# Samples' attention scores in two column halves, and the scan's output finished in its own chunk

## The reference, cut to what matters

```python
# samples (DEC_BATCH 8, DEC_SEQ 4, 16 heads of 64): attention over the cached keys and the new ones
logits = einsum('bthd,btjhd->bthj', q, kg) * ATTN_SCALE + bias
m = max(logits); pr = exp(logits - m); den = sum(pr)
o = einsum('bthj,btjhd->bthd', pr, vg) / den[..., None]

# prompt: state-space scan in chunks of 128 tokens (8 chunks), 16 heads of 64, state 128, 2 groups
y_diag = einsum('bcijgr,bcjgrp->bcigrp', cb[..., None] * decay * dtc[:, :, None], xc)
y_off  = einsum('bcign,bcigr,bcgrpn->bcigrp', cc, exp(cum), h_prev)
y = (y_diag + y_off) + xs * d_skip[:, None]
y = y.reshape(b, t, D_SSM) * silu(z)
yg = y.reshape(b, t, 2, D_SSM // 2)
yg = yg * rsqrt(mean(yg * yg, axis=-1, keepdims=True) + EPS)
h = x + concat(attn_o, yg * ssm_norm) @ w_out
y = h + square(relu(rmsnorm(h) @ w_up)) @ w_down
```

## Time and profile before

| | |
|---|---|
| runs | 2103.23, 2101.59, 2103.22 us, median 2103.22 |
| profiled execution, own time | 2098.7 us |
| its span, first to last instruction | 2096.9 us |
| PE busy | 1998.9 us (95%) |
| DVE, ACT, POOL busy | 1031.3, 699.6, 941.6 us |
| mean granted TensorE clock | 0.987 of full speed |

### The profile page before, as it was taken

The page is one execution under the profiler, slowest core; times in us unless marked ns, Lnnn a source line. Parts: engine busy times, 40 slices in busy tenths (PEclk is TensorE's granted clock), DMA queues, the critical chain, the costliest instruction groups (busy, mean ns, idle before and its releaser), DMA issues.

```text
span 2096.9 us, 30132 instructions
## 1 busy us (share of the span) xinstructions
PE 1998.9 (95%) x11992; PEld 1820.7 (87%) x11992; DVE 1031.3 (49%) x1355; ACT 699.6 (33%) x1194; POOL 941.6 (45%) x580
## 2 busy tenths in 40 slices
PE   8999999988888999899999999999999999999999
PEld 7999998777777888565567799999999999999998
DVE  4888803877767666477777561521212212121212
ACT  5344323666556676555552021210010101010010
POOL 4688613777657665234332123233332323232332
PEclk9999999999999999999999999999999999999999
DMA  4444435453343442878755423011111111111112
GB/s 168 149 190 160 149 113 127 115 121 101 87 112 95 117 132 81 267 258 277 232 210 191 172 99 126 31 51 41 51 40 50 40 50 41 49 40 50 40 50 93
DMA packets 117925, 239.36 MB, mean 114 GB/s; under 512 B 29995, under 2 KB 63659, under 8 KB 116284
## 3 DMA queue, kind: packets, MB, share of 16 engines
q1 hardware_dynamic: 94956, 205.69, 30.4%
q10 hardware_dynamic: 22864, 32.25, 4.7%
HBM read 187.78 MB, written 58.67 MB: 118 GB/s over the span
## 4 chain that ended last, share of the span: by engine, by line
PE 65%; DVE 7%; ACT 6%; issue 4%; POOL 1%; DMA 0%; ACTq 0%; DVEq 0%; SPq 0%; POOLq 0%
PE wo_psa L2377 9%; PE wo_psa L2395 9%; PE wo_psb L2377 9%; PE wo_psb L2395 7%; PE dense_ps L966 6%; PE wo_psa L2225 4%; PE sa_s L1512 3%; PE wo_psb L2329 2%; PE wo_psa L2329 2%; DVE att_p L1071 1%; PE att_t_ps L995 1%; ACT att_p L1165 1%; PE ssd_in L1616 1%; PE att_s_ps L984 1%; ACT att_qhi L1182 1%
## 5 line engine op out<-in xcount | busy, mean ns | idle before, releaser
L913 POOL TENSOR_SCALAR att_p<-att_p,att_rden 128x128 f32<-128x128 f32 (+7 forms) x128 | 251.0, 1969 | 132.6 <-DVE att_rden L1053 132.6
L2134 POOL CAST wo_hi<-wo_raw 128x1024 fp32r<-128x1024 f32 x64 | 66.7, 1042 | 496.8 <-issue 242.1
L2492 ACT ACTIVATE r_sq<-stage 128x1056 f32<-128x1056 f32 x32 | 34.8, 1089 | 625.1 <-DVE stage L2693 625.1
L2136 POOL TENSOR_TENSOR wo_lo<-wo_raw,wo_hi 128x1024 fp32r<-128x1024 f32 x64 | 185.3, 2895 | 5.1
L1058 DVE TENSOR_TENSOR att_pTlo<-att_t_ps,att_pThi 128x512 fp32r<-128x512 f32 x192 | 106.3, 554 | 112.1 <-ACT att_pThi L1173 110.6
L2377 PE MATMUL wo_psb<-mix_split,wo_hi 128*128 128x352 f32 x768 | 144.9, 323 | 0.0
L2377 PE MATMUL wo_psa<-mix_split,wo_hi 128*128 128x352 f32 x768 | 144.2, 322 | 0.0
L1173 ACT ACTIVATE att_pThi<-att_t_ps 128x512 fp32r<-128x512 f32 x192 | 93.4, 487 | 127.9 <-PE att_t_ps L995 120.7
L966 PE MATMUL dense_ps<-u_hi,w_hi 128*128 128x352 f32 x480 | 117.8, 347 | 16.4 <-DVE conv_pre L1085 7.8
L2377 PEld LDWEIGHTS wo_psb<-mix_split,wo_hi 128*128 128x128 f32 x768 | 128.3, 188 | 0.5 <-issue 0.5
L2377 PEld LDWEIGHTS wo_psa<-mix_split,wo_hi 128*128 128x128 f32 x768 | 128.0, 188 | 0.0
(11 more groups left out here) (315 smaller groups left out, 5148.0 us busy)
## 6 DMA issues: line engine op xcount, KB each, us to landing
sa_k<-in_cache_k SPq DMA_DIRECT2D x32, 640.0 KB, 7.6
sa_v<-in_cache_v SPq DMA_DIRECT2D x40, 512.0 KB, 4.7
w_raw<-in_w_feat SPq DMA_DIRECT2D x36, 512.0 KB, 6.3
wo_raw<-in_w_up SPq DMA_DIRECT2D x32, 512.0 KB, 3.5
wo_raw<-in_w_down SPq DMA_DIRECT2D x32, 512.0 KB, 3.5
out_qk<-proj_out SPq DMA_DIRECT2D x16, 528.0 KB, 7.9
tmp_bias_rows<-tmp_table ACTq DMA_DIRECT2D x8, 1024.0 KB
att_bias<-tmp_bias_rows SPq DMA_DIRECT2D x16, 512.0 KB, 3.2
```

Of the source, the lines that this page charges most:

```text
L913: pool.tensor_scalar(slot(h, qt), slot(h, qt), rden[:, qt, :], None, ALU.mult).then_inc(normed, 1)
L2136: pool.tensor_tensor(w_lo[:, j], raw_w, w_hi[:, j].bitcast(F32), ALU.subtract).then_inc(f_split[j], 1)
```

## The change

- **Scores in two column halves.** Pair f = 2u goes to rows 0 to 63 of `s_ps`, pair 2u+1 to rows 64 to 127, which are the upper 64 columns of PE's array. The column piece is the outer loop now, so the two matmuls that follow each other write different halves. The number of matmuls and their sizes are the same. `softmax_min` adds the halves: one more DVE operation, a `tensor_tensor` of 64 x 672 that adds the upper rows to the bias, ahead of the old one.
- **y in its own chunk.** `turn_y(n, g)`, `add_skip(n, g)`, `gate(n)`, `square(n)`, `sum_squares(n)` stand in iteration n, not n+1; `skip_x(n)` comes earlier on POOL. Nothing of chunk 7 but `sum_squares`, `norm_sums` and `keep_norm` is left for the head of `outward`.
- **Order.** `norm_sums(n-1)` moves between the scores and `sample_gather(n-1)` behind them; on DVE `keep_own(n-1)` opens the iteration and `softmax_min(n)` stands ahead of `keep_norm` and `keep_out`; on ACT the first two of the four `segment` calls of chunk n+1 stand ahead of `exponent(n)`, the last two behind `square(n)`; SP loads z first and the rows of decays one chunk further ahead.
- **Reciprocals.** `keep_norm` has no reciprocal. Eight reciprocals of 128 x 256 stand in `outward` at q = 8, 10, ..., 22, behind the square root, and `scale` moves to q = 25, 29, ..., 53.

```diff
@@ sync
-                if n >= 1 and n + 1 < NC:
-                    load_rows(n + 1)
+                if n:
+                    load_z(n)
                 if n + 1 < NC:
                     load_k(n + 1)
-                if n:
-                    load_z(n)
+                if n + 2 < NC:
+                    load_rows(n + 2)
@@ tensor
-                for i in range(KP):
-                    f = u * KP + i
-                    for c, w in ((0, 512), (512, NKEYS - 512)):
-                        mm = pe.matmul(s_ps[0:R, c:c + w], q_diag[:, f, :], kT[:, u, i, c:c + w],
-                                       start=(f == 0), stop=(f == NPAIR - 1))
+                for c, w in ((0, 512), (512, NKEYS - 512)):
+                    for i in range(KP):
+                        f = u * KP + i
+                        mm = pe.matmul(s_ps[i * R:(i + 1) * R, c:c + w], q_diag[:, f, :], kT[:, u, i, c:c + w],
+                                       start=(f < KP), stop=(f >= NPAIR - KP))
...
                 if n:
                     sample_scores(n, 1)
+                    sample_scores(n, 2)
+                    norm_sums(n - 1)
+                    sample_scores(n, 3)
                     sample_gather(n - 1)
-                    turn_y(n - 1, 0)
-                    sample_scores(n, 2)
-                    turn_y(n - 1, 1)
-                    sample_scores(n, 3)
...
                 sample_values(n, 1)
+                turn_y(n, 0)
...
                 sample_values(n, 3)
-                if n:
-                    norm_sums(n - 1)
+                turn_y(n, 1)
                 sample_values(n, 4)
@@ gpsimd
+                skip_x(n)
                 if n + 1 < NC:
                     place(n + 1)
-                if n:
-                    sum_squares(n - 1)
-                if n + 1 < NC:
                     weigh_x(n + 1)
-                if n + 1 < NC:
-                    skip_x(n)
+                    sum_squares(n)
@@ scalar
                 for t in range(VS):
                     cast_v(n, t)
+                if n + 1 < NC:
+                    segment(n + 1, 0)
+                    segment(n + 1, 1)
                 if n:
-                    square(n - 1)
                     exponent(n)
...
-                    for q in range(4):
-                        segment(n + 1, q)
+                square(n)
+                if n + 1 < NC:
+                    segment(n + 1, 2)
+                    segment(n + 1, 3)
@@ vector
-                dve.wait_ge(norm_kept, n + 1)
-                dve.reciprocal(part, part)
...
-                dve.tensor_tensor_reduce(out=probs[:, 0:NKEYS], in0=s_ps[0:R, 0:NKEYS], in1=bias[:], scale=1.0, scalar=3e38,
-                                         op0=ALU.add, op1=ALU.min, accum_out=low[:]).then_inc(biased, 1)
+                dve.tensor_tensor(probs[:, 0:NKEYS], s_ps[R:2 * R, 0:NKEYS], bias[:], ALU.add).then_inc(biased, 1)
+                dve.wait_ge(biased, 2 * b + 1)
+                dve.tensor_tensor_reduce(out=probs[:, 0:NKEYS], in0=s_ps[0:R, 0:NKEYS], in1=probs[:, 0:NKEYS], scale=1.0,
+                                         scalar=3e38, op0=ALU.add, op1=ALU.min, accum_out=low[:]).then_inc(biased, 1)
@@ outward
-    SCALE_AT = {9 + 6 * k: k for k in range(KD)}
+    INVERT_AT = {8 + 2 * i: i for i in range(8)}
+    SCALE_AT = {25 + 4 * k: k for k in range(KD)}
...
+            def invert_root(i):
+                part = y_sums[:, i // 4, i % 4 * 2 * P:(i % 4 + 1) * 2 * P]
+                dve.wait_ge(y_rooted, 2)
+                dve.reciprocal(part, part).then_inc(y_rooted, 1)
```

More of the change, by code:

```diff
@@ L1672, in _ @@
                 sample_values(n, 3)
-                if n:
-                    norm_sums(n - 1)
+                turn_y(n, 1)
                 sample_values(n, 4)
-            pe_tail = turn_y, sample_gather, norm_sums
-            mixed.pe_tail = pe_tail
+            mixed.pe_tail = sample_gather, norm_sums
         @block.gpsimd
@@ L1762, in _ @@
                     kit.clear(pool)
-            mixed.pool_tail = skip_x, sum_squares
+            mixed.pool_tail = sum_squares
         @block.scalar
@@ L1970, in _ @@
                     split_v(n, 1)
+                    softmax_min(n)
+                    keep_norm(n - 1)
                     keep_out(n - 1)
-                    add_skip(n - 1, 0)
-                    add_skip(n - 1, 1)
-                    gate(n - 1)
-                    split_v(n, 2)
-                    softmax_min(n)
                 add_state(n, 0)
@@ L1986, in _ @@
                     split_v(0, 1)
-                    split_v(0, 2)
+                split_v(n, 2)
+                if n == 0:
                     split_new()
-                split_v(n, 3)
                 if n + 1 < NC:
                     mask_cb(n + 1)
+                add_skip(n, 0)
+                split_v(n, 3)
+                add_skip(n, 1)
                 split_v(n, 4)
-                if n + 1 < NC:
-                    mix(n + 1, 0)
-                if n + 1 < NC:
-                    keep_own(n)
-                    mix(n + 1, 1)
-                    scale_off(n + 1, 0)
-                    if n:
-                        keep_norm(n - 1)
-            mixed.dve_tail = keep_own, add_skip, gate, keep_out, keep_norm
+                gate(n)
+            mixed.dve_tail = keep_own, keep_out, keep_norm
     return mixed
@@ L2106, in _ @@
         def _(pool):
-            skip_x, sum_squares = mixed.pool_tail
+            sum_squares = mixed.pool_tail
             pool.wait_ge(mixed.k_used, mixed.scores)
@@ L2256, in grown @@
                 mm.then_inc(state_made, 1)
-            turn_y, sample_gather, norm_sums = mixed.pe_tail
+            sample_gather, norm_sums = mixed.pe_tail
             last = mixed.chunks - 1
@@ L2261, in _ @@
             pe.wait_ge(mixed.state_summed, 2 * mixed.chunks)
-            turn_y(last, 0)
             for k in range(KD):
@@ L2265, in _ @@
                 step(k, (0, 1))
-                if k == 0:
-                    turn_y(last, 1)
                 if k == 1:
                     sample_gather(last)
-                if k == 5:
+                if k == 3:
                     norm_sums(last)
@@ L2408, in cast_a @@
                 act.activation(m_hi[:, k, 0:SEQ], stage[:, k % 3, 0:SEQ], ACT.Copy).then_inc(a_hi_made, 1)
-            square = mixed.act_tail
             act.wait_ge(mixed.k_used, mixed.scores)
@@ L2420, in _ @@
             cast_a(3)
-            square(mixed.chunks - 1)
             cast_a(4)
@@ L2561, in scale @@
                                          op1=ALU.mult).then_inc(y_scaled, 1)
-            keep_own, add_skip, gate, keep_out, keep_norm = mixed.dve_tail
+            keep_own, keep_out, keep_norm = mixed.dve_tail
             last = mixed.chunks - 1
             split_a(0)
-            split_a(1)
             keep_own(last)
-            add_skip(last, 0)
-            split_a(2)
-            add_skip(last, 1)
-            gate(last)
+            for k in range(1, 4):
+                split_a(k)
             keep_out(last)
-            split_a(3)
             split_a(4)
-            keep_norm(last - 1)
-            split_a(5)
-            split_a(6)
-            split_a(7)
             keep_norm(last)
+            for k in range(5, KD):
+                split_a(k)
             dve.wait_ge(as_made, 1)
```

24 lines of the change are left out of this document (14 added, 10 removed).

## The result

| | median (lowest to highest) | runs | profiled execution's span | mean clock |
|---|---|---|---|---|
| before | 2102.40 us (2099.95 to 2103.23) | 4 | 2096.9 us | 0.987 |
| after | 2135.41 us (2133.26 to 2135.96) | 4 | 2134.1 us | 0.959 |

The ratio is 1.0157 with a 95% interval of 1.0139 to 1.0175: slower by 33 us, outside the range of the prediction (2085 to 2121), and the sign is wrong too.

The account below looks back on a forecast made before the run. PE's own stream was taken as the bound. Seven periods at -2.05 us gave -14.4; edges and clock (+2.0 + 1.5 + 3.0 - 1.7 + 0.5 + 1.0) made it -8.1, so 2095.1 us from 2103.2; range 2085 to 2121.

Parts of the forecast that it names:

- Scores: PE's score blocks overlap in part: 1.51 us a block, 6.04 a sample instead of 9.64, 3.6 us saved a period.
- rival 2: Full overlap of the scores on PE: 4.82 us a sample, another 1.2 us a period, 2086.7 us; chance 17%.
- The pairing by neighbours: Scores on PE: in the order A1 A2 B1 B2 only A2 and B1 pair up, giving 1.51 us a block.
- The wait before the last values: PE idles 2.05 us ahead of `sample_values(n, 4)`, behind the second turn of y and DVE's skip and split.
- The gap before the scores: PE's gap ahead of the first score block: 0.8 us instead of 1.32, 0.5 us won a period.
- Softmax and state hidden: New DVE operation taken as 0.8 us; exponentials at 13.8 us, PE wants them at 15.7: hidden, 1.9 us to spare.
- A period at full clock: One iteration of the loop: 29.22 - 3.6 - 0.5 + 2.05 = 27.2 us.
- Clock: PE's clock in the loop: 1 us in all for an odd half-clock stretch from the new idle of 2.05 us.
- Rival 3: Idle PE halves the clock for 3 to 5 us every iteration, costing 1.7 to 2.5 us a period: 2108 us; chance 9%.
- Edges: Outside the periods: iteration 0 +2.0 and +1.5, chunk 7 +3.0, head of `outward` -1.7, projection +0.5 us.
- the forecast's first premise: PE's own stream is the bound in the loop: busy 27.66 of 29 us, period 29.22 us.

Follow-up runs that it names:

- pieces apart: The changed kernel with the scores' two column pieces inside the pair again (lower half 512, lower 160, upper 512, upper 160): 2134.5 us, ratio 1.0166 to before.
- order 2: Kernel before with column halves, reciprocals in the projection and a new order on DVE, PE and ACT (second y turn between inner and second states): 2090.2 us.

## Why the prediction was wrong

- **Scores: right mechanism, undersized.** Forecast 1.51 us a block and 6.04 a sample; measured 1.28 and about 5.0 (1.28 + 2.41 + 1.28), near the full overlap of rival 2 (4.82). The pairing by neighbours that I assumed is not needed: with the pieces apart blocks are as short. The rule that weight loads overlap only in another row group (the Trainium skill, TensorE: Matmul & The Clock Gate, Part 3, The mechanism), doubted in the prediction, does not hold for these two column halves, or nothing would have been won; the Trainium skill's 2.38 times for three tiles (same page, Part 3, Measured speedup) is 79%, here 9.64/5.0 = 1.93 times for two is 96%.
- **The wait before the last values: right.** 2.05 forecast; measured in all 8 iterations, up to 2.55, 2.48 on average, with `sa_vlo` as releaser. The 0.5 is the split that waited for POOL (1.74 instead of 1.22).
- **The gap before the scores: wrong.** 0.8 forecast, 2.03 at full clock: the gate ahead of the copy takes 2.92 us, not 1.14.
- **Softmax and state hidden: this step failed.** I counted PE's time up to the turn of the probabilities as cover, and gave the softmax no cost. That overlooks `add_state(n, 0)`, which stands behind the softmax on DVE and which PE's second states wait for, ahead of that turn. Splits of 4.06 us and one more operation make it late: a wait of 1.54 us in the iterations shown, 9.9 us in the loop, where the forecast has none.
- **A period at full clock**: 27.2 - 1.1 (scores) + 0.5 + 1.2 + 1.5 = 29.3, measured 29.6. DVE's durations were taken from rows where POOL did not work beside them; the change moved the gate beside POOL's `weigh_x` and the splits beside its `skip_x`.
- **Clock: this step failed most.** I put 1 us, and gave half clock in every iteration 9%, at 1.7 to 2.5 us a period. Against the fast iteration of 29.6 the six others lost 4.6 to 5.8 us, 30 us together, nearly all of the 32.0. I compared one new wait with two waits of before; the three waits of a period add up to 4.8 to 6.1 us. Rival 3 was too small as well: it had a stretch of 3 to 5 us at half clock, and a usual period has 13.6 us of it, in two stretches. That waiting matters is shown, since fillers in the three waits brought 1.00 back; how much of it makes the clock fall is not.
- **Edges: nearly right.** Up to the first `sa_own` +7.9 us against 2.0 + 1.5 and the 3.0 of a chunk's turns and wait, 6.5; behind the last -2.7 against -1.7 + 0.5. No wait of PE in the loop is put down to a DMA or a reciprocal, as said.

So the forecast's first premise fell: PE was the bound only as long as it was full. Taking 4.6 us from it made the ring through DVE's list the bound, at 29.2 us in the old order and 29.6 in the new, so nothing was won at full clock. PE now waited within each period, its clock fell, and the work of PE that is on the ring took 4.6 us longer.

## What to carry to other kernels

Before shortening the busiest engine, close the ring of the second one: add its durations and hand-overs for one period, with the part of PE's work that it waits for. What PE saves beyond that is not time but idle PE, and here idle PE came with a lower clock and cost more than it saved. When an operation with two SBUF inputs moves on DVE, look at what POOL does at its new place. If a filler of unused matmuls makes a kernel faster, the order is what to mend: order 2, without fillers, has the halves and takes 10 us less than the kernel before.

## What the hardware showed that I had not expected

- Two float32 matmuls of 64 stationary columns in different column halves run side by side, both passes: 16 matmuls of 512 and 160 columns in 5.0 instead of 9.64 us, with each single record as long as before (608 and 602 ns).
- With waits of 0.7, 1.5 and 2.5 us in a period the granted clock was 0.80; at the same wait of 1.54 us it fell in one iteration and not in the next. Summed waits of 26.7, 28.2 and 27.4 us in three kernels went with 0.99, 0.95 and 0.89.
- DVE's operations with two SBUF inputs ended about one normal duration after the POOL operation beside them: 1.22 became 2.92 us, two of 0.69 became 3.92.
